# Moving the routing work, the u-row gathers and their dot products of one decoder layer to other keys

## The chip, the cores and the metric

The kernel runs on one core of a Trainium2 chip. Five engines work side by side, each with its own instruction stream: PE (TensorE, matmuls), DVE (VectorE), ACT (ScalarE), POOL (GpSimd) and SP (SyncE, which here only issues DMAs). They wait for each other and for DMAs by semaphores. The metric is the device time of one execution in microseconds (us).

## The reference, cut to what matters

The layer takes 256 tokens of width 1024 through a recurrent branch and attention, cross-attention, and then a channel mixer over 16,384 single-neuron experts. Only the mixer matters here:

```
q = (t @ w_q).reshape(T, 8, 2, 128)                 # 8 heads, two halves
s = einsum('thpd,hpnd->thpn', q, sub_keys)          # 128 sub-keys a half
s_top, i_top = top_k(s, 16)                         # then 16 of the 16 x 16 sums
best_s, pos = top_k(cand_s, 16); ids = take(cand_i, pos); gates = softmax(best_s)
act = gelu(einsum('td,ted->te', x_c, u[ids_c]), approximate=False)
y = einsum('te,ted->td', g_c * act, v[ids_c])       # 128 experts a token
```

An expert number is a pair (i, j) of sub-keys, each 0 to 127. All of it is float32.

## The kernel before, in words

**Dense stages.** Most of the mixer is computed for all experts: the u stage multiplies all u rows with the tokens, key by key (a key j is 128 experts), and the v stage multiplies all v rows with the weighted activations, again key by key. In both, SP loads a key's 512 KB (`raw`, four slots), ACT copies it to a high part (`split_high`), DVE subtracts to get the low part (`split_low`), and PE multiplies both. DVE's iteration j splits key j + 4, and a slot is free again when PE is done with its key, so ACT and DVE run at most four keys ahead. In the u stage ACT then applies GeLU (`gelu`) to what PE leaves in PSUM.

**Routing.** DVE finds the experts of each token meanwhile: four parts a head (`route_part`; two top-16 of 128, one of 256, one of index arithmetic), 8 heads, two tiles of 128 tokens, 64 parts in all. The first 14 come ahead of the u stage; part n of the others comes in DVE's iteration `part_key(n)`, 1.5 keys apart. When a batch of heads is done (`BATCHES`), ACT takes the exponentials (`gate_exp`, `batch_key` + 2, which needs another activation table than GeLU) and DVE makes the gates and addresses (`gates`, `batch_key` + 4).

**Where the gates go.** Three ways, by token. For most, POOL scatters the gates with indirect DMAs (L517, 128 elements each) into a zeroed map in HBM (`wmap`): 16 scatters for each of 8 heads of tile 0, then 4 for each head of tile 1. From the second head on, a head's first scatter of a set waits until those of the head before have landed. SP (and, for the first two blocks, POOL) reads the map back as `wblk`, and DVE weighs the activations with it (`weigh`); the first `weigh` stands in iteration 124 of the u stage. For 48 tokens, PE places the gates by one-hot matrices: 12 groups of 4 (`onehots_i` on DVE and `onehots_j` on ACT two keys ahead, `route` on PE behind key `ROUTE0` + 3g, `place` on DVE in the same key), after PE has transposed the routing rows behind key `WEAVE` (80), which waits for the last gates.

**Sparse tokens.** For 48 tokens the v side is done by gathering single v rows (48 gathers of 128 rows, `vg`, three buffers) and adding them with a weight on DVE (`sparse_fma`, from v iteration 12 on). For 16 of them the u side is done so too: 16 gathers of 128 u rows (`u_rows` on POOL, 512 KB each, buffers `ug0` and `ug1`), each followed by one dot product with the tokens (`u_dot` on DVE). `u_rows(0)` waits for the index lists, which go through HBM (SP, at raw keys 88 and 93), and for the tokens' rows times the gains (DVE at `XREP_KEY`, semaphore `s_xg`); from the third on each waits for the dot that frees its buffer. Before, they stand behind every second scatter of the last batch (heads 3 to 7 of tile 1), the last six behind all scatters, and the dots come at keys 92 to 120.

**Order.** Each engine's instructions run in the order written, so what waits holds all behind it. On POOL: scatters with the u gathers among them, the first two `wblk`, eight gathers of stored activations (`act_rows`), then v rows and more activation gathers in turn.

Of the kernel before, what the change touches and what calls it, by code (L numbers as in the profile page):

```python
# [22 lines left out]
P = 128  # L23
# [36 lines left out]
GRP = 4  # L60
# [20 lines left out]
BATCHES = ((0, 0, 1), (0, 1, 3), (0, 3, 5), (0, 5, PH), (1, 0, 3), (1, 3, PH))  # L81
EARLY = 2
PARTS0 = 14
WEAVE = 80
LATE0 = 76
RUN = 7
GAINS = 6
ROUTE0 = 84
RSTEP = 3
HALVES_TO = 80  # L90
XREP_KEY, DOT0 = 90, 92
NUG = 2


def build(nc, x, mem, par, wa, wx, w, keys_t, u_t, urow, v, g_row, wmap, adump, sgate, sidx, xres, xrows, out):
    ctx = ExitStack()
    with ctx:
# [189 lines left out]

        def part_key(n):

            return -(-3 * (n - PARTS0 + 1) // 2) - 1  # L290

        def set_ranks(ap, k):

# [36 lines left out]

        SPARSE = ((P - NS, NSA, 0, NDA), (P - NSB, NSB, NDA, NDB))

        def placed(j):

            return GRP * max(0, min(NGRP, (j - ROUTE0) // RSTEP + 1))

        def group_at(j):

            g, rest = divmod(j - ROUTE0, RSTEP)
            return g if rest == 0 and 0 <= g < NGRP else None  # L340

        def dot_key(c):

            return DOT0 + 15 * c // 8

        ug = (ug0, ug1)

# [4 lines left out]
        def _(sp):  # L352
# [42 lines left out]
            for j in range(4, KEYS):  # L395
                sp.wait_ge(s_ul, j - 3)
                sp.dma_start(raw[:, j // 2 % 2, j % 2], u_t[j // 2][:, j % 2]).then_inc(s_raw[j % 4], 16)
                if j == 88:
                    sp.wait_ge(s_stg, 1)
                    for far, near in ((sgate, stage_g), (sidx, stage_i)):  # L400
                        for t0, nt, c0, nc_ in SPARSE:
                            sp.dma_start(far[P * c0:P * (c0 + nc_), :].rearrange("(r t c) o -> t r (c o)", t=nt, c=nc_),
                                         near[t0:t0 + nt, :].rearrange("t (r c) -> t r c", c=nc_)).then_inc(s_sst, 16)
                if j == XREP_KEY:
                    sp.wait_ge(s_rt, TT * PH)
                    sp.wait_ge(s_xrd, 16)
                    for r in range(P // NSB):
                        sp.dma_start(xrep[NSB * r:NSB * r + NSB], xrows).then_inc(s_xrb, 16)
                    sp.dma_start(ug0[:], g_row.broadcast_to([P, D])).then_inc(s_xrb, 16)
                if j == 93:  # L410
                    sp.wait_ge(s_sst, 64)
                    for far, near in ((sgate, gate_s), (sidx, idx_v)):
                        for t0, nt, c0, nc_ in SPARSE:
                            sp.dma_start(near[:, c0:c0 + nc_],
                                         far[P * c0:P * (c0 + nc_), :].rearrange("(p c) o -> p (c o)", p=P)).then_inc(s_sbk, 16)
                if j % DUMP == 0 and j >= 3 * DUMP:
                    dump(j - 3 * DUMP, j - 2 * DUMP)
                if j == KEYS - 4:
                    dump(KEYS - 3 * DUMP, KEYS - 2 * DUMP)
# [37 lines left out]
        def _(pool):  # L457
# [41 lines left out]
            def u_rows(c):  # L499
                if c == 0:  # L500
                    pool.wait_ge(s_sbk, 64)
                    pool.wait_ge(s_xg, 1)
                if c >= NUG:
                    pool.wait_ge(s_dot, c - NUG + 1)
                nc.gpsimd.indirect_dma_start(out=ug[c % NUG][:], out_offset=None, in_=urow,
                                             in_offset=bass.IndirectOffsetOnAxis(ap=idx_v[:, NDA + c:NDA + c + 1], axis=0)).then_inc(s_ug[c % NUG], 16)

            pool.wait_ge(s_zero, 16 * NZERO)
            for b, (t, h0, h1) in enumerate(BATCHES):
                pool.wait_ge(s_gr, b + 1)  # L510
                for h in range(h0, h1):
                    for k in TILE_SETS[t]:
                        nr = SETS[k][3]
                        if h:
                            pool.wait_ge(s_sca[k], 16 * nr * h)
                        for r in range(nr):
                            nc.gpsimd.indirect_dma_start(  # L517
                                out=wmap, out_offset=bass.IndirectOffsetOnAxis(ap=set_ranks(widx, k)[:, h, r:r + 1], axis=0),
                                in_=set_ranks(gate, k)[:, h, r:r + 1], in_offset=None, compute_op=ALU.add).then_inc(s_sca[k], 16)
                            if b == len(BATCHES) - 1 and r % 2:  # L520
                                u_rows((nr * (h - h0) + r) // 2)

            for c in range(2 * (BATCHES[-1][2] - BATCHES[-1][1]), NDB):
                u_rows(c)
            for k, (_, _, _, nr) in enumerate(SETS):
                pool.wait_ge(s_sca[k], 16 * nr * PH)
            pool.wait_ge(s_sst, 64)
            for p in range(2):
                nc.gpsimd.dma_start(wblk[:, p], wm[:, WBK * p:WBK * p + WBK]).then_inc(s_wbp[p], 16)
            pool.wait_ge(s_ad, 16 * KEYS // DUMP)  # L530
            pool.wait_ge(s_ix, 1)

# [16 lines left out]
        def _(act):  # L549
# [304 lines left out]
            for j in range(KEYS):  # L854
                landed = 16 * ((j + 4) // 4 + 1)
                if j == XRT_KEY:
                    act.wait_ge(s_xd, 16)
                    act.wait_ge(s_xrd, 16)
                gelu(j)
                if j < KEYS - 4:  # L860
                    split_high(j % 4, landed, (s_um, j + 1), s_uh)
                elif j < KEYS - 1:
                    split_high(j % 4, landed, (s_um, j + 1), s_vh, second=True)
                if exps < len(BATCHES) and j == batch_key(exps) + 2:
                    gate_exp(exps)
                    exps += 1
                if j == WEAVE:
                    act.wait_ge(s_kt, 1)
                    nc.scalar.activation(kt3[:], acc[:, 2, 0:3 * P].rearrange("p (a t) -> p a t", a=3)[:, :, HT:HT + OT], ACT.Copy).then_inc(s_kte, 1)
                    act.wait_ge(s_kte, 1)  # L870
                if group_at(j + 2) is not None:
                    onehots_j(group_at(j + 2))
                if j == KEYS - 3:
                    act.wait_ge(s_gw, NGRP)
                    for p in range(2):
                        a_high(p)

            split_high(3, 16 * (KEYS // 4 + 1), (s_um, KEYS), s_vh, second=True)
            for p in (2, 3):
                a_high(p)  # L880
            act.wait_ge(s_dot, NDB)
            nc.scalar.activation(aw_s[:, NDA:NSD], dots[:], ACT.Gelu).then_inc(s_dg, 1)
            act.wait_ge(s_fx, KEYS - ROUTE0)
            for j in range(KEYS - 4):
                split_high(j % 4, 16 * (KEYS // 4 + (j + 4) // 4 + 1), (s_vm, j + 1), s_vh, second=True)
                if j % 2 and (j + 7) // 2 < NWB:
                    a_high((j + 7) // 2)
            warm_sqrt()
            act.wait_ge(s_Wl, NWB)
            for c in range(DC):  # L890
# [27 lines left out]
        def _(dve):  # L918
# [339 lines left out]
            def place(g):  # L1258

                dve.wait_ge(s_gm, g + 1)  # L1260
                j0, c = ROUTE0 + RSTEP * g, P + group_token(g)
                dve.wait_ge(s_ua, j0)
                w = acc[:, 2 + g % 2].rearrange("p (t j) -> p j t", t=GRP)
                aw = act_w[:, :, c:c + GRP]
                V.tensor_copy(aw[:, j0:KEYS], w[:, j0:KEYS])
                V.tensor_tensor(aw[:, 0:j0], w[:, 0:j0], aw[:, 0:j0], ALU.mult).then_inc(s_gw, 1)
# [59 lines left out]
                    V.tensor_scalar(to, vg[:, c % NVG], w, None, ALU.mult).then_inc(s_fma, 1)  # L1326

            def u_dot(c):
                dve.wait_ge(s_ug[c % NUG], 16 * (c // NUG + 1))
                row = ug[c % NUG]  # L1330
# [3 lines left out]
            parts, batches, dot = PARTS0, EARLY, 0  # L1334
            for j in range(KEYS):
                if j < HALVES_TO:
                    split_low_halves(j % 4, s_ul, (s_uh, j + 5))
# [1 line left out]
                    split_low(j % 4, s_ul, (s_uh, j + 5))  # L1339
                elif j < KEYS - 1:  # L1340
                    split_low(j % 4, s_vl, (s_vh, j + 5 - KEYS), second=True)
                if batches < len(BATCHES) and j == batch_key(batches) + 4:
                    gates(batches)
                    batches += 1
                if parts < 4 * TT * PH and j == part_key(parts):
# [11 lines left out]
                if j == DOT0 - 1:  # L1357
                    dve.wait_ge(s_sbk, 64)
                    V.tensor_scalar(idx_a[:], idx_v[:, 0:NDA], float(NSA), tcol[:, 2:3], ALU.mult, ALU.add).then_inc(s_ix, 1)
                if dot < NDB and j == dot_key(dot):  # L1360
                    u_dot(dot)
                    dot += 1
                if group_at(j + 2) is not None:
                    onehots_i(group_at(j + 2))
                if j == KEYS - 4:
# [12 lines left out]
            for j in range(KEYS - 4):  # L1378
# [6 lines left out]
                split_low(j % 4, s_vl, (s_vh, j + 5), second=True)  # L1385
                if j % 2 == 0 and 4 <= (j + 6) // 2 < NWB:
                    a_low((j + 6) // 2)
                if c < NSD and j == fma_step(c):
                    sparse_fma(c)
                    c += 1  # L1390
# [432 lines left out]
```

## Time and profile before

| | us |
|---|---|
| median of three runs | 987.94 (986.53 to 989.32) |
| the profiled execution | 987.83, its span 986.0 |
| u stage, on PE | 280.7 to 667.7 |
| v stage, on PE | 667.7 to 972.2 |
| busy: PE, DVE, ACT, POOL | 952.0, 803.7, 558.3, 421.6 |

The profile covers one execution; its times count from the first instruction. A line as L517 is a line of the kernel. A tile name left of an arrow is written, right of it is read. Durations of matmuls are modelled and overlap; the distances between their starts are sharper.

### The profile page before, as it was taken

Reading aid. Unit: us, or ns where it says so; the run is one execution under the profiler, and the core shown is the slowest. Engines: PE = TensorE matmul, PEld = TensorE weight load, DVE = VectorE, ACT = ScalarE, POOL = GpSimd, SP = SyncE. Lnnn points to the kernel's source line nnn. Section 1 sums busy time; section 2 is a strip of 40 time slices with the busy share of each in tenths; the row PEclk is TensorE's granted clock in tenths of the full one; section 3 lists DMA queues with packets and bytes.
Section 4 is the critical chain, followed back from the end, with each engine's and each line's share of the span. In section 5 each row is a group of like instructions: output and inputs, shape, how many; then the busy total and the mean of one; then the engine's idle time right before and its main releaser. Section 6 shows DMA issues by size and latency. Waiting matters only on the chain.

```text
span 986.0 us, 18901 instructions
## 1 busy us (share of the span) xinstructions
PE 952.0 (97%) x7255; PEld 927.2 (94%) x7255; DVE 803.7 (82%) x1557; ACT 558.3 (57%) x1005; POOL 421.6 (43%) x283
## 2 busy tenths in 40 slices
PE   8999999999999999999999598999999999999997
PEld 8897899999999999999999598999999999999997
DVE  5988776447999999999976377867798999989887
ACT  7675445645556555555566454755555555555455
POOL 1001001000588888888885677216365223222210
PEclk9999999999999999999999889999999999999999
DMA  9699635444557777878888588878999999999992
GB/s 318 207 334 327 235 136 204 131 129 129 175 110 192 186 195 190 197 192 202 198 223 229 126 240 228 295 233 285 307 368 347 354 342 358 336 354 358 364 314 86
DMA packets 130812, 239.90 MB, mean 243 GB/s; under 512 B 33904, under 2 KB 82800, under 8 KB 130368
## 3 DMA queue, kind: packets, MB, share of 16 engines
q1 hardware_dynamic: 96944, 204.60, 61.6%
q0 software_dynamic: 33376, 34.00, 15.6%
q8 instruction: 31, 0.51, 0.2%
q10 hardware_dynamic: 432, 0.57, 0.2%
q14 instruction: 29, 0.24, 0.1%
HBM read 223.72 MB, written 14.88 MB: 242 GB/s over the span
## 4 chain that ended last, share of the span: by engine, by line
PE 60%; POOL 26%; issue 6%; DMA 4%; DVE 3%; ACT 1%; ACTq 0%; DVEq 0%; POOLq 0%
POOL wmap L517 26%; PE acc L1720 11%; PE bank L1720 10%; PE acc L1479 10%; PE bank L1721 5%; PE acc L1721 5%; PE acc L1461 4%; DMA wmap<-gate,widx 3%; PE bank L1669 2%; PE bank L1668 2%; PE bank L1670 2%; PE acc L1462 2%; PE acc L1465 1%; DVE wsp L930 1%; PE bank L1577 1%
## 5 line engine op out<-in xcount | busy, mean ns | idle before, releaser
L517 POOL DMA_INDIRECT wmap<-gate,widx x160 | 277.3, 1733 | 95.6 <-issue 47.0
L803 ACT ACTIVATE hl<-raw 128x1024 fp32r<-128x1024 f32 x192 | 203.5, 1061 | 78.9 <-PE bank L1721 41.3
L1668 PE MATMUL bank<-xt,hl 128*128 128x240 f32 x768 | 213.9, 279 | 3.8 <-DVE hl L1187 3.5
L1670 PE MATMUL bank<-xt,hl 128*128 128x240 f32 x768 | 212.2, 276 | 0.0
L1669 PE MATMUL bank<-xt,hl 128*128 128x240 f32 x768 | 212.2, 276 | 0.0
L1180 DVE TENSOR_TENSOR hl<-raw,hl 128x1024 fp32r<-128x1024 f32 x132 | 161.7, 1225 | 56.0 <-ACT hl L803 55.5
L1668 PEld LDWEIGHTS bank<-xt,hl 128*128 128x128 f32 x768 | 146.3, 191 | 4.7 <-ACT act_s L814 4.3
L1669 PEld LDWEIGHTS bank<-xt,hl 128*128 128x128 f32 x768 | 146.2, 190 | 0.0
L1670 PEld LDWEIGHTS bank<-xt,hl 128*128 128x128 f32 x768 | 146.1, 190 | 0.0
L544 POOL DMA_INDIRECT vg<-v,idx_v x48 | 64.7, 1348 | 164.3 <-DVE acc_s L1324 143.4
L1720 PE MATMUL acc<-whl,hl 128*128 128x416 f32 x380 | 121.3, 370 | 0.0
L1720 PE MATMUL bank<-whl,hl 128*128 128x416 f32 x380 | 120.9, 368 | 0.0
L809 ACT ACTIVATE act_w<-bank 128x208 f32<-128x208 f32 (+12 forms) x128 | 42.8, 334 | 128.9 <-PE bank L1670 128.7
L554 ACT ACTIVATE wsp<-wraw 128x2048 fp32r<-128x2048 f32 x35 | 66.9, 1913 | 57.0 <-PE acc L1462 26.5
L930 DVE TENSOR_TENSOR wsp<-wraw,wsp 128x2048 fp32r<-128x2048 f32 x34 | 77.9, 2290 | 25.9 <-ACT wsp L554 25.6
L1721 PE MATMUL bank<-whl,hl 128*128 128x208 f32 x380 | 98.1, 258 | 0.0
L1721 PE MATMUL acc<-whl,hl 128*128 128x208 f32 x380 | 97.9, 258 | 0.0
L1479 PE MATMUL acc<-xt,wsp 128*128 128x256 f32 x672 | 83.9, 285 | 0.1
L1479 PEld LDWEIGHTS acc<-xt,wsp 128*128 128x128 f32 x672 | 81.6, 191 | 0.7 <-issue 0.4
L1187 DVE TENSOR_TENSOR hl<-raw,hl 128x512 fp32r<-128x512 f32 x120 | 76.6, 687 | 1.9 <-ACT hl L803 0.8
L1668 PE MATMUL bank<-xt,hl3u 128*128 128x240 f32 x256 | 70.8, 277 | 1.7 <-DVE hl3u L1187 1.7
L1721 PEld LDWEIGHTS acc<-whl,hl 128*128 128x128 f32 x380 | 72.5, 191 | 0.0
(299 smaller groups left out, 2169.8 us busy)
## 6 DMA issues: line engine op xcount, KB each, us to landing
raw<-u_t SPq DMA_DIRECT2D x128, 512.0 KB, 4.6
raw<-v SPq DMA_DIRECT2D x128, 512.0 KB, 5.9
wmap<-zeros SPq DMA_DIRECT2D x5, 2048.0 KB, 11.2
wblk<-wmap SPq DMA_DIRECT2D x62, 160.0 KB, 5.9
wraw<-w_in SPq DMA_DIRECT2D x9, 1024.0 KB, 9.4
wraw<-w_pq SPq DMA_DIRECT2D x8, 1024.0 KB, 5.3
wraw<-w_ck SPq DMA_DIRECT2D x4, 1024.0 KB, 8.9
wraw<-w_cv SPq DMA_DIRECT2D x4, 1024.0 KB, 6.2
```

The source lines that it names most:

```text
L517: nc.gpsimd.indirect_dma_start(out=wmap, out_offset=bass.IndirectOffsetOnAxis(ap=set_ranks(widx, k)[:, h, r:r + 1], axis=0), in_=set_ranks ...
L554: nc.scalar.activation(wsp[:, u % 2, 0], wraw[:, u % WRAW], ACT.Copy).then_inc(s_wh, 1)
L803: nc.scalar.activation(eslot(k, 0, second), raw[:, k // 2, k % 2], ACT.Copy).then_inc(ready, 1)
L930: V.tensor_tensor(wsp[:, u % 2, 1], wraw[:, u % WRAW], wsp[:, u % 2, 0].bitcast(F32), ALU.subtract).then_inc(s_wl, 1)
L1180: V.tensor_tensor(eslot(k, 1, second), raw[:, k // 2, k % 2], eslot(k, 0, second).bitcast(F32), ALU.subtract).then_inc(ready, 1)
L1187: last = V.tensor_tensor(eslot(k, 1, False)[:, q], raw[:, k // 2, k % 2, q], eslot(k, 0, False)[:, q].bitcast(F32), ALU.subtract)
L1479: last = pe.matmul(dst, a, b, start=(c == c0 and n == 0), stop=(c == c1 - 1 and n == 2))
L1668: pe.matmul(dst, uh[:, c], xt[:, c, 0, 0:UT], start=(c == 0), stop=False)
L1669: pe.matmul(dst, uh[:, c], xt[:, c, 1, 0:UT], start=False, stop=False)
L1670: last = pe.matmul(dst, ul[:, c], xt[:, c, 0, 0:UT], start=False, stop=(c == DC - 1))
L1720: pe.matmul(both, vh[:, q], whole, start=first, stop=False, skip_group_check=True)
L1721: last = pe.matmul(both[:, 0], vl[:, q], whole[:, 0], start=False, stop=False, skip_group_check=True)
```

## The change

Parts come every 1.6 keys in place of 1.5. The exponentials of a batch come one key behind its last part (two before), the gates three (four before). The transposes move from key 80 to 83, the groups to 87 + 2.75g (84 + 3g before). SP stores and reloads the lists at raw keys 92 and 97 (88 and 93), the product with the gains moves from key 90 to 91. Twelve u gathers stand behind the scatters 2, 5, 8, ... of tile 1 (counted from 0), their dots at keys 97 to 122; the other four stand behind the first two `wblk`, use one buffer, and have their dots in the v stage at iterations 1, 4, 7 and 10. ACT's GeLU of the dots moves to v iteration 20.

```diff
-WEAVE = 80
+WEAVE = 83
-ROUTE0 = 84
-RSTEP = 3
+ROUTE0 = 87
-XREP_KEY, DOT0 = 90, 92
+XREP_KEY = 91
+DOT_KEYS = (97, 100, 103, 106, 108, 110, 112, 114, 116, 118, 120, 122)
+LATE_DOTS = (1, 4, 7, 10)
+U_AFTER = (2, 5, 8, 11, 13, 15, 17, 20, 22, 25, 28, 31)
...
         def part_key(n):
-            return -(-3 * (n - PARTS0 + 1) // 2) - 1
+            return -(-8 * (n - PARTS0 + 1) // 5) - 1
...
+        def group_key(g):
+            return ROUTE0 + 11 * g // 4
...
+        def uslot(c):
+            return c % NUG if c < len(DOT_KEYS) else 0
...
-                if j == 88:
+                if j == 92:
                     sp.wait_ge(s_stg, 1)
...
-                if j == 93:
+                if j == 97:
                     sp.wait_ge(s_sst, 64)
...
-                if c >= NUG:
+                if c >= len(DOT_KEYS):
+                    pool.wait_ge(s_dot, c)
+                elif c >= NUG:
                     pool.wait_ge(s_dot, c - NUG + 1)
...
-                            if b == len(BATCHES) - 1 and r % 2:
-                                u_rows((nr * (h - h0) + r) // 2)
-
-            for c in range(2 * (BATCHES[-1][2] - BATCHES[-1][1]), NDB):
-                u_rows(c)
+                            if t and nr * h + r in U_AFTER:
+                                u_rows(U_AFTER.index(nr * h + r))
...
                 nc.gpsimd.dma_start(wblk[:, p], wm[:, WBK * p:WBK * p + WBK]).then_inc(s_wbp[p], 16)
+            for c in range(len(DOT_KEYS), NDB):
+                u_rows(c)
...
-                if exps < len(BATCHES) and j == batch_key(exps) + 2:
+                if exps < len(BATCHES) and j == batch_key(exps) + 1:
                     gate_exp(exps)
...
+                    act.wait_ge(s_dot, len(DOT_KEYS))
                     for p in range(2):
                         a_high(p)
...
-                if batches < len(BATCHES) and j == batch_key(batches) + 4:
+                if batches < len(BATCHES) and j == batch_key(batches) + 3:
                     gates(batches)
...
-                if dot < NDB and j == dot_key(dot):
-                    u_dot(dot)
-                    dot += 1
+                if j in DOT_KEYS:
+                    u_dot(DOT_KEYS.index(j))
...
+                if j in LATE_DOTS:
+                    u_dot(len(DOT_KEYS) + LATE_DOTS.index(j))
```

## Rows read from the trace of the kernel before

**Rows 1.** Page, parts 1 and 5: busy; count, total us, mean ns, idle before.

```profile
PE 952.0 (97%) x7255; PEld 927.2 (94%) x7255; DVE 803.7 (82%) x1557; ACT 558.3 (57%) x1005; POOL 421.6 (43%) x283
...
L517 POOL DMA_INDIRECT wmap<-gate,widx x160 | 277.3, 1733 | 95.6 <-issue 47.0
```

**Rows 2.** Waits of the u stage: waiter, releaser; us in total, times, longest.

```profile
DVE ug L1331 <- DMA ug<-u,idx_v: 19.5, 5, 12.7
...
ACT krow L795 <- DVE krow L1219: 1.9, 3, 1.2
```

**Rows 3.** Timeline of PE: start, duration, line, operation; in brackets idle before.

```profile
508.67 0.55 PE L1703 MATMUL acc<-ident,krow 128*128 128x128 f32 x3 [1.57 <-DVE widx L1245]
...
569.32 2.08 PE L1693 MATMUL acc<-oh_j,oh_i 128*128 128x128 f32 x8 [13.50 <-DVE oh_i L1254]
...
578.41 0.27 PE L1668 MATMUL bank<-xt,hl3u 128*128 128x240 f32 x1
...
581.10 1.05 PE L1693 MATMUL acc<-oh_j,oh_i 128*128 128x128 f32 x8
581.91 0.36 PE L1668 MATMUL bank<-xt,hl 128*128 128x240 f32 x1
...
602.18 1.93 PE L1693 MATMUL acc<-oh_j,oh_i 128*128 128x128 f32 x8 [3.00 <-DVE oh_i L1254]
...
607.49 0.27 PE L1668 MATMUL bank<-xt,hl3u 128*128 128x240 f32 x1
...
667.70 0.35 PE L1720 MATMUL acc<-whl,hl 128*128 128x416 f32 x1
...
708.54 0.36 PE L1720 MATMUL acc<-whl,hl 128*128 128x416 f32 x1
```

**Rows 4.** Windows: stretch, busy PE, PEld, DVE, ACT, POOL, then clock, DMA, GB/s.

```profile
280.00:504.00 224.00, 218.53 (x1934) 217.12 (x1933) 214.37 (x616) 128.81 (x257) 190.46 (x111) 1.00 0.78 192
...
602.00:604.00 2.00, 1.82 (x9) 1.82 (x10) 2.00 (x4) 0.00 (x0) 1.73 (x1) 0.59 0.61 145
```

**Rows 5.** Timeline of POOL: scatters of tile 1, then the start of the v stage.

```profile
522.72 1.55 POOL L517 DMA_INDIRECT wmap<-gate,widx  x1 [0.30 <-issue]
529.63 1.55 POOL L517 DMA_INDIRECT wmap<-gate,widx  x1 [5.36 <-DMA wmap<-gate,widx]
...
540.21 1.85 POOL L517 DMA_INDIRECT wmap<-gate,widx  x1 [3.41 <-DMA wmap<-gate,widx]
...
552.11 1.55 POOL L517 DMA_INDIRECT wmap<-gate,widx  x1 [4.34 <-DMA wmap<-gate,widx]
...
670.85 1.03 POOL L535 DMA_INDIRECT aw_s<-adump,idx_a  x1 [25.75 <-DMA adump<-act_s]
...
683.90 0.98 POOL L544 DMA_INDIRECT vg<-v,idx_v  x1 [0.30 <-issue]
```

**Rows 6.** Tiles: u gathers' ns; landings of late u, first v, first weight blocks.

```profile
L505 POOL DMA_INDIRECT ug<-u,idx_v x16: 939/1416/1820, 555.8 to 642.2; - x16
...
DMA to landing us min/median/max: 4.8/6.5/7.5
...
DMA to landing us min/median/max: 7.6/8.1/9.6
...
DMA to landing us min/median/max: 6.0/6.1/6.2
```

**Rows 7.** Timeline of DVE: a head's parts, the product, the first sparse sum.

```profile
481.28 0.17 DVE L1211 TENSOR_SCALAR posu<-topi 128x16 uint32<-128x16 uint32 x1
...
497.39 0.17 DVE L1211 TENSOR_SCALAR posu<-topi 128x16 uint32<-128x16 uint32 x1
...
541.42 1.22 DVE L1356 TENSOR_TENSOR xrep<-xrep,ug 128x1024 f32<-128x1024 f32 x1
...
702.94 0.76 DVE L1326 TENSOR_SCALAR acc_s<-vg,w_s 128x1024 f32<-128x1024 f32 x1
...
704.01 1.22 DVE L1180 TENSOR_TENSOR hl<-raw,hl 128x1024 fp32r<-128x1024 f32 x1
```

More of the change, by code:

```diff
@@ L331, in build, with uslot_use @@
         SPARSE = ((P - NS, NSA, 0, NDA), (P - NSB, NSB, NDA, NDB))
+        def group_key(g):
+            return ROUTE0 + 11 * g // 4
         def placed(j):
-            return GRP * max(0, min(NGRP, (j - ROUTE0) // RSTEP + 1))
+            return GRP * sum(1 for g in range(NGRP) if group_key(g) <= j)
         def group_at(j):
[L339 to L344, printed above, removed]
+            return next((g for g in range(NGRP) if group_key(g) == j), None)
+        def uslot(c):
+            return c % NUG if c < len(DOT_KEYS) else 0
+        def uslot_use(c):
+            return sum(1 for k in range(c + 1) if uslot(k) == uslot(c))
         ug = (ug0, ug1)
@@ L502, in u_rows @@
                     pool.wait_ge(s_xg, 1)
-                if c >= NUG:
+                if c >= len(DOT_KEYS):
+                    pool.wait_ge(s_dot, c)
+                elif c >= NUG:
                     pool.wait_ge(s_dot, c - NUG + 1)
-                nc.gpsimd.indirect_dma_start(out=ug[c % NUG][:], out_offset=None, in_=urow,
-                                             in_offset=bass.IndirectOffsetOnAxis(ap=idx_v[:, NDA + c:NDA + c + 1], axis=0)).then_inc(s_ug[c % NUG], 16)
+                nc.gpsimd.indirect_dma_start(out=ug[uslot(c)][:], out_offset=None, in_=urow,
+                                             in_offset=bass.IndirectOffsetOnAxis(ap=idx_v[:, NDA + c:NDA + c + 1], axis=0)).then_inc(s_ug[uslot(c)], 16)
             pool.wait_ge(s_zero, 16 * NZERO)
@@ L880, in _ @@
                 a_high(p)
-            act.wait_ge(s_dot, NDB)
-            nc.scalar.activation(aw_s[:, NDA:NSD], dots[:], ACT.Gelu).then_inc(s_dg, 1)
             act.wait_ge(s_fx, KEYS - ROUTE0)
@@ L887, in _ @@
                     a_high((j + 7) // 2)
+                if j == 20:
+                    act.wait_ge(s_dot, NDB)
+                    nc.scalar.activation(aw_s[:, NDA:NSD], dots[:], ACT.Gelu).then_inc(s_dg, 1)
             warm_sqrt()
@@ L1260, in place @@
                 dve.wait_ge(s_gm, g + 1)
-                j0, c = ROUTE0 + RSTEP * g, P + group_token(g)
+                j0, c = group_key(g), P + group_token(g)
                 dve.wait_ge(s_ua, j0)
@@ L1328, in u_dot @@
             def u_dot(c):
-                dve.wait_ge(s_ug[c % NUG], 16 * (c // NUG + 1))
-                row = ug[c % NUG]
+                dve.wait_ge(s_ug[uslot(c)], 16 * uslot_use(c))
+                row = ug[uslot(c)]
                 V.scalar_tensor_tensor(row[:], row[:], 1.0, xrep[:], ALU.mult, ALU.mult,
                                        accum_out=dots[:, c:c + 1]).then_inc(s_dot, 1)
-            parts, batches, dot = PARTS0, EARLY, 0
+            parts, batches = PARTS0, EARLY
             for j in range(KEYS):
@@ L1356, in _ @@
                     V.tensor_tensor(xrep[:], xrep[:], ug0[:], ALU.mult).then_inc(s_xg, 1)
-                if j == DOT0 - 1:
+                if j == XREP_KEY + 1:
                     dve.wait_ge(s_sbk, 64)
                     V.tensor_scalar(idx_a[:], idx_v[:, 0:NDA], float(NSA), tcol[:, 2:3], ALU.mult, ALU.add).then_inc(s_ix, 1)
-                if dot < NDB and j == dot_key(dot):
-                    u_dot(dot)
-                    dot += 1
+                if j in DOT_KEYS:
+                    u_dot(DOT_KEYS.index(j))
                 if group_at(j + 2) is not None:
```

## The prediction, made before the changed kernel ran

> **What bounds the kernel now.** I read the page first: TensorE is busy for 952.0 of 986.0 us [rows 1], so only its gaps can be won, and then whatever makes them. The waits of the u stage come next: DVE waited 19.5 us in five waits for u rows that POOL gathers, 12.7 us in one of them [rows 2]. TensorE's timeline says what these waits cost [rows 3]. A key of the u stage takes 2.69 us there (578.41 to 581.10) and a routing group behind it 0.81 us (581.10 to 581.91). The group behind key 96 waited 13.50 us for its one-hots, the one behind key 105 waited 3.00 us, and the transposes of the routing rows behind key 80 waited 1.57 us for the last gates. Up to key 80 the gaps are small: 224 less 218.53, 5.5 us, in one stretch of 224 us [rows 4]; DVE and TensorE have almost the same pace there, since four routing parts and six splits took 16.11 us on DVE (481.28 to 497.39) [rows 7] against six keys of 2.69 us, 16.1 us. The v stage begins at 667.70 and its key 17 at 708.54, 2.40 us a key, with no gap [rows 3]. So about 27 us of gaps lie ahead of the v stage, and the v stage itself has none to give.
>
> All times below are on the clock of the profiled execution, which took 987.8 us with a span of 986.0; the median of the runs is 987.9, the same within their scatter. About 0.3%, 3.0 us, is what a measurement can tell from no change.
>
> **Parts every 1.6 keys.** No work is removed; six keys become 6.4 for a head. DVE's 16.11 us grow by 0.4 split of some 1.2 us to 16.6 us, against 17.2 us of TensorE: 0.6 us of lead for each head, 1.8 us between two sets of gates that stand three heads apart. That is about what one set costs now (5.5 us in three sets, some 1.8 us each). Against it, the exponentials of a batch now run on ACT one key behind the batch's last part and no longer two, and ACT already waited 1.9 us in three waits for that part [rows 2]; while ACT stands, the next splits stand too. I count nothing. The ends are a gain of all 5.5 us and a loss of twice the present 1.9 us, 3.8.
>
> **Gates and transposes.** The last part moves from key 74 to 79, the last gates from 78 to 82, the transposes only from 80 to 83. TensorE waited 1.57 us with two keys between the two; with one key it is 2.69 more, and DVE has two keys without parts ahead of the gates in place of three, so it comes with about 1 us less lead: 5.2 us, 3.6 more than now. After the 3.00 us wait behind key 105 the granted clock stood at 0.59 (near the 1.2 GHz level) in the next 2 us [rows 4], and group and key took 5.31 us (602.18 to 607.49) in place of 3.50: 1.8 us. After the wait of 1.57 us it stayed full. A wait of 5.2 us brings this 1.8 us too: 5.4 us together. The ends are nothing, if DVE has caught up, and 8.
>
> **The first u gather.** It stands behind the third scatter of tile 1 and needs the index lists and the product of the gains, which DVE forms at key 91. Scatters of tile 1 start no later than now, and the third is out by 522.7, where the fourth starts now [rows 5]. The product started at 541.42 in key 90 [rows 7]. In the new order it comes 2.69 later (one key), 5.4 later (above), and 1.6 earlier (one group less has run, 0.81, and no group is placed in this key, some 0.8): 547.9, and it takes 1.22, so 549.1. POOL stands for 26 us with 29 scatters and the gathers queued behind it. Before, it scattered in this time.
>
> From there POOL is the chain. 29 scatters take 2.0 us each (1.73 mean and 0.30 of issue [rows 1]), 58.0; 12 gathers 1.72 (1.42 and 0.30 [rows 6]), 20.6. At each of seven changes of head POOL waits until the head before has landed; where no gather lies between, it now waits 5.36, 3.41 and 4.34 us [rows 5], 4.1 more than the issue, and five changes are of that kind: 20.4. The other two have a gather between; I give them 1 us each. That is 101.0 us, to 650.1 for the twelfth gather; the last scatter starts 3.7 earlier, 646.4, lands some 5.6 later (2.0 and a wait of 3.6 to 4.3), 652.0. Only then can the first blocks of weights be fetched, 6.1 us [rows 6], 658.1; weighing and splitting them takes about 2.5 us, and the v stage starts at 660.6. TensorE alone would be done sooner: from the product's key it has 37 keys of 2.69 and ten groups, some 108 us after 543, 651. The twelve dots cost nothing of their own up to key 116; the last three wait for their gathers inside this difference of 9 us. So the removed 13.5 and 3.0 us and their slow clock come back partly as a wait at the end: 660.6 against 667.70, **7.1 us won**. The ends: 19 us won, if the product is early and the landings short, and 1 lost.
>
> **Four dots in the v stage.** They use one buffer, so each gather waits for the dot before it, and now the gathers for the sparse v rows queue behind all four. Relative to the start of the v stage, DVE's split of key 17 starts at 36.3 (704.01 [rows 7]); twelve iterations earlier, at 2.40 a key, iteration 1 splits at 7.5. The dot behind it ends at 10.0. The gather of the next lands 6.5 later [rows 6], 16.5, about when iteration 4 comes to it; dot done 17.8. Landing 24.3, while iteration 7 was ready at some 23.7; dot done 25.5. With the fourth gather issued POOL is free at 27.2. Now the eight gathers of stored activations and the first of v: 13.05 us between 670.85 and 683.90 [rows 5], to 40.3, and 8.1 to land [rows 6], 48.4. In the profile of before this whole chain began at 3.15. The first sparse sum is due at 35.2 (702.94). Sum and weighing take 1.07 and the split of key 17 1.2: ready at 50.7, while TensorE wants key 17 at 40.8 (708.54): 9.9 us of wait, in which nothing else is queued for TensorE. Then again 1.8 us of slow clock: **11.7 us lost**. The v stage runs at TensorE's pace to its end, so nothing gives it back. The ends are 2 us and 15 us.
>
> A rule of the Trainium skill speaks against this term. Rows of before: the last u gathers landed in 4.8, 6.5, 7.5 us (least, median, most), the first v gathers in 7.6, 8.1, 9.6 [rows 6]. The page "DMA: Bandwidth & Descriptors", section "Anatomy of one DMA", puts a transfer from this queue at 2.0 us and its bytes over 436 GB/s, which is 3.2 us for 512 KB, an estimate by that page. By that the gathers would wait for no dot, and the v rows be there early enough that a small wait of about 2 us remained, as in the third rival. The rows don't bear it out; the sum goes by them.
>
> **Dot and one-hot keys, groups from 87 every 2.75 keys.** Twelve groups as before, 0.81 us each on TensorE, and the same instructions of DVE and ACT at other keys; the dots that now come late were the ones between which DVE waited. Nothing, with half a microsecond to either side.
>
> **Sum.** 987.8 − 7.1 + 11.7 = 992.4; I say 992.3.
>
> **Rivals.**
> *DVE arrives with lead.* If the slower pace hides the gates' 5.5 us and the transposes wait no longer than now, the product comes 10.9 us earlier and the whole POOL chain with it: 992.3 − 10.9 = 981.4, faster. For it: 0.6 us a head. Against: the exponentials moved towards their part, and one key between gates and transposes. It decides at key 83: a wait under 2 us there.
> *Shorter landings.* With 4.8 us for the late u gathers (the shortest shown), v rows at 7.6, and 3.4 us at the changes of head, the v stage starts 3.5 us earlier and its wait is 2.2 us shorter: 986.6, no change. For it: the three waits at heads lie 2 us apart, and the shortest is 3.41 [rows 5]. Against: v gathers took longer than u gathers [rows 6].
> *Fast gathers.* At 3.2 us for all gathers the v chain ends with a wait of some 2 us at full clock: 992.3 − 9.7 = 982.6. This is the time that the cited rule gives. Against: the shortest of the late u gathers took 4.8 [rows 6].
> *The gathers don't go among the scatters.* If DVE were still waiting at key 97 for its first row, 13 us would stay: the forecast plus some 7, 999. The gather lands some 7 us after the product, the dot is due six keys, 16 us, after it; I hold this for unlikely.
>
> **How the numbers follow.** Forecast 0.50 (its own range 989 to 997), lead 0.13, fast gathers 0.07, shorter landings 0.27, no weave 0.03. Faster is the second and third, 0.20; same 0.27 (the landings); slower 0.53. The range 982 to 999 leaves out the far side of the early product, and double losses.
>
> **What would show it.** Transposes behind key 83 waiting 4 to 6 us; POOL idle from 522 to about 549 ahead of its first gather; no TensorE gap between keys 87 and 117; the last scatter at about 646; v stage from 658 to 663; then one gap of TensorE of some 10 us ahead of key 16 to 18 of the v stage, released by DVE waiting at its first sparse sum for a v row. If TensorE runs through the v stage without that gap, the forecast is wrong by its largest term; if the v stage starts before 653, by its second.

## The result, and the profile after

The changed kernel takes 992.99 us (median of five runs, 989.31 to 993.41) against 987.94 us (five runs, 985.87 to 989.32): a ratio of 1.0046, with an interval of 1.0024 to 1.0069. It is slower by half a percent, near the 992.3 us forecast. The profiled execution took 993.41 us with a span of 991.6 us, 5.6 us longer than before.

| start of | before | after | difference |
|---|---|---|---|
| u stage | 280.74 | 281.23 | +0.5 |
| key 80 of tile 1 | 504.25 | 505.15 | +0.9 |
| v stage | 667.70 | 664.29 | −3.4 |
| last matmuls of the v stage | 972.19 | 978.06 | +5.9 |

So the u stage won 3.4 us and the v stage lost 9.3 (313.77 us long in place of 304.49). First the page of the changed kernel, parts 1 and 5, in the columns of [rows 1]:

```profile
PE 959.0 (97%) x7255; PEld 933.0 (94%) x7255; DVE 802.3 (81%) x1554; ACT 556.8 (56%) x1002; POOL 428.0 (43%) x283
...
L528 POOL DMA_INDIRECT wmap<-gate,widx x160 | 273.2, 1708 | 99.0 <-issue 47.8
```

The count of TensorE's instructions is the same, and its busy time grew by 7 us: the same matmuls, some of them at the lower clock. The waits of the changed kernel from 280 to 720 us (waiter, releaser; us in total, times, longest) show where it stood:

```profile
POOL ug L516 <- DVE ug L1344: 38.4, 7, 15.8
POOL ug L516 <- DVE xrep L1369: 31.2, 1, 31.2
DVE ug L1344 <- DMA ug<-u,idx_v: 20.7, 4, 8.2
...
ACT krow L806 <- DVE krow L1232: 10.2, 4, 3.6
...
PE acc L1734 <- DVE hl L1193: 6.1, 1, 6.1
...
PE acc L1717 <- DVE widx L1258: 5.2, 1, 5.2
```

DVE waits for u rows as long as before (20.7 against 19.5 us in [rows 2]), only later. ACT's wait for routing parts has grown from 1.9 to 10.2 us. New is the 31.2 us that POOL stands for the product. TensorE's timeline of the changed kernel has one line for each loss:

```profile
521.22 0.90 PE L1717 MATMUL acc<-ident,krow 128*128 128x128 f32 x3 [5.15 <-DVE widx L1258]
...
642.40 0.57 PE L1682 MATMUL bank<-xt,hl3u 128*128 128x240 f32 x1 [2.69 <-DVE hl3u L1193]
...
653.27 0.57 PE L1682 MATMUL bank<-xt,hl 128*128 128x240 f32 x1 [3.70 <-DVE hl L1193]
...
664.29 0.35 PE L1734 MATMUL acc<-whl,hl 128*128 128x416 f32 x1
...
711.75 0.72 PE L1734 MATMUL acc<-whl,hl 128*128 128x416 f32 x1 [6.15 <-DVE hl L1193]
```

The 13.50 and 3.00 us ahead of the one-hot groups in [rows 3] are gone: no group waits any more. In their place stand 5.15 us at the transposes, 2.69 and 3.70 us in the last keys of the u stage, and 6.15 us in the v stage. Each of the four is followed by slow matmuls: the transposes took 0.90 us where they took 0.55. Windows of the changed kernel (columns of [rows 4]; the clock stands behind POOL's share) around the transposes show the same:

```profile
280.00:504.00 224.00, 218.41 (x1930) 216.76 (x1929) 209.87 (x601) 125.20 (x254) 188.66 (x113) 1.00 0.77 194
...
516.00:518.00 2.00, 0.07 (x1) 0.00 (x0) 1.96 (x2) 2.00 (x5) 1.70 (x2) 1.00 0.88 197
...
522.00:524.00 2.00, 2.00 (x11) 2.00 (x11) 0.42 (x1) 0.29 (x1) 0.00 (x0) 0.50 0.47 78
524.00:526.00 2.00, 2.00 (x12) 2.00 (x11) 0.00 (x0) 0.00 (x0) 0.00 (x0) 0.50 0.96 311
526.00:528.00 2.00, 2.00 (x19) 2.00 (x19) 0.00 (x0) 1.11 (x3) 0.00 (x0) 0.96 0.92 207
```

TensorE stood from 516 to 521; after that it is busy without a break, but until 526 with 11 or 12 matmuls in 2 us in place of 19, at a granted clock of 0.50 (1.2 GHz). The first line says that the small gaps up to key 80 are what they were: 224 less 218.41, 5.6 us, against 5.5 in [rows 4].

DVE's timeline of the changed kernel shows what the two waits in the last keys of the u stage come from, the tenth and the eleventh dot (keys 118 and 120):

```profile
639.98 1.23 DVE L1344 SCALAR_TENSOR_TENSOR ug<-ug,xrep 128x1024 f32<-128x1024 f32 x1 [8.16 <-DMA ug<-u,idx_v]
...
650.85 1.23 DVE L1344 SCALAR_TENSOR_TENSOR ug<-ug,xrep 128x1024 f32<-128x1024 f32 x1 [7.12 <-DMA ug<-u,idx_v]
```

POOL's timeline of the changed kernel, from the third scatter of tile 1 to the first sparse v row:

```profile
519.97 1.55 POOL L528 DMA_INDIRECT wmap<-gate,widx  x1 [0.31 <-issue]
552.75 1.13 POOL L516 DMA_INDIRECT ug<-u,idx_v  x1 [31.23 <-DVE xrep L1369]
...
559.93 1.54 POOL L528 DMA_INDIRECT wmap<-gate,widx  x1 [4.16 <-DMA wmap<-gate,widx]
...
648.52 1.55 POOL L528 DMA_INDIRECT wmap<-gate,widx  x1 [0.30 <-issue]
...
652.22 1.17 POOL L538 DMA_DIRECT2D wblk<-wmap  x2 [0.85 <-DMA wmap<-gate,widx]
...
673.78 1.75 POOL L516 DMA_INDIRECT ug<-u,idx_v  x1 [15.85 <-DVE ug L1344]
683.38 0.95 POOL L516 DMA_INDIRECT ug<-u,idx_v  x1 [7.85 <-DVE ug L1344]
689.77 1.68 POOL L516 DMA_INDIRECT ug<-u,idx_v  x1 [5.44 <-DVE ug L1344]
691.75 1.74 POOL L546 DMA_INDIRECT aw_s<-adump,idx_a  x1 [0.30 <-issue]
...
704.52 0.95 POOL L555 DMA_INDIRECT vg<-v,idx_v  x1 [0.30 <-issue]
```

In [rows 5] the stored activations were fetched from 670.85 and the v rows from 683.90, 3.15 and 16.20 us into the v stage. Now three late gathers, each behind the dot before it, stand ahead of them, and they come at 27.5 and 40.2 us. The chain of waits of the changed kernel (start, us, what) walks the same road back:

```profile
642.93 7.89 DMA ug<-u,idx_v
...
673.78 8.07 DMA ug<-u,idx_v
...
704.52 4.79 DMA vg<-v,idx_v
709.40 0.75 DVE acc_s L1339
```

All three are landings of gathers: that of the eleventh dot's rows, near the end of the u stage, that of a late dot's, and that of the first v row. The tiles of the changed kernel: landings of the u gathers after 650 us, of the first v rows, and the first weighing.

```profile
DMA to landing us min/median/max: 4.2/7.4/8.1
...
DMA to landing us min/median/max: 4.8/5.1/5.9
...
L1322 DVE TENSOR_TENSOR act_w<-act_w,wblk x2: 483/484/485, 658.3 to 658.7; 128x320 f32<-128x320 f32 x2
```

### The profile page after: what moved, and what is told of

Read it like the earlier page. It is cut to its first block, busy times and chain, and to the rows that moved or that the text cites. A ratio compares the mean times of both kernels' runs of the same rounds, so it can differ in the third digit from the quotient of the medians.

```text
span 991.6 us, 18892 instructions
## 1 busy us (share of the span) xinstructions
PE 959.0 (97%) x7255; PEld 933.0 (94%) x7255; DVE 802.3 (81%) x1554; ACT 556.8 (56%) x1002; POOL 428.0 (43%) x283
## 4 chain that ended last, share of the span: by engine, by line
PE 70%; DVE 16%; DMA 4%; ACT 3%; POOL 3%; issue 3%; ACTq 0%; DVEq 0%; POOLq 0%
PE acc L1493 14%; PE acc L1734 9%; PE bank L1734 9%; PE bank L1682 5%; PE bank L1683 5%; PE bank L1684 5%; DVE hl L1200 5%; PE bank L1735 4%; PE acc L1735 4%; PE acc L1475 4%; PE acc L1476 2%; DMA wmap<-gate,widx 2%; DVE hl3u L1200 2%; DMA ug<-u,idx_v 2%; POOL wmap L528 1%
## 5 line engine op out<-in xcount | busy, mean ns | idle before, releaser
L528 POOL DMA_INDIRECT wmap<-gate,widx x160 | 273.2, 1708 | 99.0 <-issue 47.8
L555 POOL DMA_INDIRECT vg<-v,idx_v x48 | 74.2, 1545 | 137.6 <-DVE acc_s L1337 129.8
L820 ACT ACTIVATE act_w<-bank 128x208 f32<-128x208 f32 (+11 forms) x128 | 43.0, 336 | 125.4 <-PE bank L1684 125.2
L862 ACT ACTIVATE whl<-act_w 128x416 fp32r<-128x416 f32 x64 | 35.1, 551 | 76.3 <-DVE act_w L1322 76.1
```

The costliest lines, as they stand in the source:

```text
L528: nc.gpsimd.indirect_dma_start(out=wmap, out_offset=bass.IndirectOffsetOnAxis(ap=set_ranks(widx, k)[:, h, r:r + 1], axis=0), in_=set_ranks ...
L555: nc.gpsimd.indirect_dma_start(out=vg[:, c % NVG], out_offset=None, in_=v, in_offset=bass.IndirectOffsetOnAxis(ap=idx_v[:, c:c + 1], axis= ...
```

## The experiments

Each alters the changed kernel in one or two places, except where it says otherwise; the kernel before, run beside them, took 988.2 and 988.0 us. The changed kernel was not run beside them, so a difference from its 992.99 us is one between sittings. A time is a median, a trace one execution, which can lie some us off the median; where that matters, the text says so.

**Groups from key 85.** Two more keys between the last gates and the transposes.

```diff
-WEAVE = 83
+WEAVE = 85
```

> The changed kernel with the transposes behind key 85 in place of 83, nothing else. Theory (the transposes stand one key too close to the gates; their wait of 5.15 us and the slow clock of key 84 push the product of key 91 and with it the whole POOL chain): two keys, 5.4 us, cover the wait; TensorE's gap behind the transposes under 0.5 us, no slow key, the first u gather near 545.5 in place of 552.8, v stage from 657, same gap in the v stage; 986 us. Rival (the v stage's start is set by the scatters' own landings and not by the product): the gap goes, the v stage still starts at 664, 993 us.

It took 985.08 us, 0.9973 [0.9953, 0.9994] of the time before, in ten runs from 982.01 to 991.25. In the profiled one (988.88 us, 3.8 above the median) the transposes started at 521.07 without a wait, and the first gather at 544.91 in place of 552.75; POOL now waited for the index lists, which landed about 0.2 us behind the product. Of these 7.8 us only 4.9 reached the v stage, which started at 659.43, later than expected: four of the last dots waited for their gathers, and behind the first of them (6.17 us) one group stood, as this line of TensorE's timeline in that run shows.

```profile
621.88 2.08 PE L1707 MATMUL acc<-oh_j,oh_i 128*128 128x128 f32 x8 [4.24 <-DVE oh_i L1267]
```

So the wait at key 83 delays POOL's chain by its length and the slow matmuls behind it. In this execution the next wait on the chain hides part of what its removal wins; by the medians the kernel gained 7.9 us, all of it, so the hidden part is shown for this execution only.

**u gathers later among the scatters.**

```diff
-U_AFTER = (2, 5, 8, 11, 13, 15, 17, 20, 22, 25, 28, 31)
+U_AFTER = (11, 13, 15, 17, 19, 21, 23, 25, 27, 29, 30, 31)
```

> The changed kernel with the twelve u gathers behind scatters 11, 13, 15, ... 29, 30, 31 of tile 1 in place of 2, 5, 8, ... Theory (the first gather held POOL for 31 us with 29 scatters behind it): POOL scatters through from 520, waits for the product only some 5 us, the last scatter starts near 630 in place of 648.5, the v stage starts at 653 to 655 set by TensorE's own keys, the gap in the v stage stays near 6 us; 982 to 984 us. Rival (the late dots wait for landings and for each other, whatever the order on POOL): v stage from 662 to 665, 991 to 994 us.

982.62 us, 0.9941 [0.9919, 0.9962]. POOL scatters while it waited before, and stands 3.77 us for the product, not 31.23. TensorE's timeline of that run:

```profile
520.91 0.90 PE L1717 MATMUL acc<-ident,krow 128*128 128x128 f32 x3 [5.16 <-DVE widx L1258]
...
652.66 0.35 PE L1734 MATMUL acc<-whl,hl 128*128 128x416 f32 x1
...
700.22 0.71 PE L1734 MATMUL acc<-whl,hl 128*128 128x416 f32 x1 [6.49 <-DVE hl L1193]
```

The transposes wait as before it, the two waits of 2.69 and 3.70 us are gone, and the v stage starts 11.6 us earlier. The gap of the v stage is untouched. The place of the gathers among the scatters, not their number, cost these 11.6 us.

**Stored activations ahead of the late gathers.**

```diff
-            for c in range(len(DOT_KEYS), NDB):
-                u_rows(c)
+            u_rows(len(DOT_KEYS))
...
-            act_rows(0, ACTB)
+            act_rows(0, 4)
+            u_rows(len(DOT_KEYS) + 1)
+            act_rows(4, ACTB)
+            u_rows(len(DOT_KEYS) + 2)
...
+                if c == NVG - 1:
+                    u_rows(len(DOT_KEYS) + 3)
```

> The changed kernel with POOL's order at the start of the v stage altered: four gathers of stored activations behind the first late u gather, four behind the second, the first three v gathers ahead of the fourth; the same transfers in all. Theory (the v gathers are late because they queue behind four u gathers that each wait for a dot): the first v row lands by 30 us after the start of the v stage, before it is due at 35; no gap near key 17; 984 us. Rival (the late rows share the DMA engines with the loads of the v stage, so the rows come late in any order): a gap of 4 us or more stays, 989 us or more.

987.1 us, 0.9991 [0.9968, 1.0014]: no difference from the kernel before, and between the two theories. The first v row was fetched 21.9 us into the v stage (683.40, from a start at 661.53) in place of 40.2, and no sparse sum waited for it. But the dots, which come every third iteration, now wait for their own gathers; DVE's timeline of that run:

```profile
680.64 1.23 DVE L1348 SCALAR_TENSOR_TENSOR ug<-ug,xrep 128x1024 f32<-128x1024 f32 x1 [4.03 <-DMA ug<-u,idx_v]
...
697.92 1.23 DVE L1348 SCALAR_TENSOR_TENSOR ug<-ug,xrep 128x1024 f32<-128x1024 f32 x1 [3.01 <-DMA ug<-u,idx_v]
```

TensorE stood 2.61 us behind the second, again with slow matmuls after it. With this order too somebody waits; whether another order of four dots within ten iterations on one buffer would do without was not tried.

**The late dots spread over the v stage.**

```diff
-LATE_DOTS = (1, 4, 7, 10)
+LATE_DOTS = (1, 20, 40, 60)
...
-            for c in range(len(DOT_KEYS), NDB):
-                u_rows(c)
+            u_rows(len(DOT_KEYS))
...
+                if c in (4, 12, 20):
+                    u_rows(len(DOT_KEYS) + 1 + (4, 12, 20).index(c))
...
-                if j == 20:
+                if j == 70:
```

> The changed kernel with its four dots of the v stage at iterations 1, 20, 40 and 60 in place of 1, 4, 7 and 10, the u gathers of the last three behind the v gathers 4, 12 and 20 on POOL, and ACT's gelu of these dots at key 70. Theory (the gap ahead of v key 17 comes from POOL, which stands for the dots before it may fetch stored activations and sparse v rows): the gap of 6.15 us and the slow clock behind it vanish, the v stage is as long as in the kernel before (304.5 us in place of 313.8), and the kernel takes about 984 us. Rival (the u gathers cost the v stage in whatever place, because their 512 KB hold up the v rows and blocks of weights): the waits move to sparse sums behind these gathers, with gaps of 2 us and more, 988 us or more.

981.79 us, 0.9934 [0.9911, 0.9956]. One window of that run over the v stage, in the columns of [rows 4]:

```profile
661.00:971.00 310.00, 310.00 (x2083) 308.28 (x2082) 276.44 (x336) 170.46 (x211) 120.60 (x83) 1.00 0.93 335
```

TensorE is busy for all 310 us at full clock. The same dots and gathers cost the v stage nothing in these places; what cost was where they stood in POOL's queue and in DVE's order, which this edit moves together. The rival falls.

**The kernel before, with its dots alone moved.** No other part of the change.

```diff
-            return DOT0 + 15 * c // 8
+            return 98 + 3 * c // 2
```

> The kernel before with one line altered: its sixteen dots at keys 98 to 120, 1.5 keys apart, in place of 92 to 120. Theory (the gap of 13.5 us came only from the first dot standing ahead of its gather, which POOL reaches at 555.8): the gap behind key 96 and its slow clock go, 16 us; later dots wait for gathers for some 5 us in all, the v stage starts at 652 to 656; 973 to 976 us. Rival (the gathers among the scatters set the pace, and what the first dot does not wait the later ones do): v stage from 663, 983 us or more.

982.62 us, 0.9941 [0.9917, 0.9966]: the rival was right, within half a us. The 13.50 us went, and came back in pieces. TensorE's timeline of the profiled execution, which took 986.70 us, the longest of six, with the v stage from 666.60:

```profile
586.23 1.64 PE L1693 MATMUL acc<-oh_j,oh_i 128*128 128x128 f32 x8 [3.11 <-DVE oh_i L1254]
...
600.04 1.77 PE L1693 MATMUL acc<-oh_j,oh_i 128*128 128x128 f32 x8 [2.96 <-DVE oh_i L1254]
...
614.94 2.08 PE L1693 MATMUL acc<-oh_j,oh_i 128*128 128x128 f32 x8 [4.05 <-DVE oh_i L1254]
...
629.51 1.16 PE L1693 MATMUL acc<-oh_j,oh_i 128*128 128x128 f32 x8 [2.53 <-DVE oh_i L1254]
```

Together 12.65 us there, and some 4 us less by the median: the gathers on POOL come as late as before (the first at 556.1), so DVE waits a little for several of them. Moving the one constant still beat the whole change.

**Groups from key 85 and later gathers together.**

```diff
-WEAVE = 83
+WEAVE = 85
...
-U_AFTER = (2, 5, 8, 11, 13, 15, 17, 20, 22, 25, 28, 31)
+U_AFTER = (11, 13, 15, 17, 19, 21, 23, 25, 27, 29, 30, 31)
```

> The changed kernel with two single edits together: routing groups from key 85 (as the run with that edit alone, 985.1 us) and the u gathers from the eleventh scatter on (alone 982.6 us). Theory (POOL's chain from the product to the last scatter is what both shorten, so they add): the product is done about 5 us earlier, POOL no longer stands for it, the v stage starts at 645 to 647 (652.7 less 6 to 7), the gap of some 6 us ahead of v key 17 is untouched, and the kernel takes about 976 us. Rival (the last dots then wait for their gathers in the u stage, as they did with the groups from key 85 alone, where one waited 6.2 us): v stage from 651 or later, 981 us or more.

973.96 us, 0.9856 [0.9823, 0.9889], 2 us better than the theory. The v stage starts at 644.98, no transpose and no dot of the u stage waits; the gap in the v stage is 5.19 us. The rival falls: the two edits add (7.9 and 10.4 us alone, 19.0 together), since each takes other waits from TensorE, the one at the transposes and the two at the last dots, with the slow matmuls behind them.

**Exponentials two keys behind their part.** With the groups from key 85, to be set beside the first experiment.

```diff
-                if exps < len(BATCHES) and j == batch_key(exps) + 1:
+                if exps < len(BATCHES) and j == batch_key(exps) + 2:
...
-                if batches < len(BATCHES) and j == batch_key(batches) + 3:
+                if batches < len(BATCHES) and j == batch_key(batches) + 4:
```

> The changed kernel with the groups from key 85, and with the exponentials of a batch two keys behind its last routing part in place of one, and the gates four keys behind in place of three; to be set beside the run with the groups from key 85 alone (985.1 us). Theory (ACT stands for DVE's last part, and DVE's next splits stand for ACT): ACT's waits for routing parts fall from 10 us to about 2, TensorE's small gaps at keys 16 to 57 of tile 1 from 5.3 us to 2 or 3, and the kernel takes about 982 us. Rival (these gaps are DVE's own pace at the gates, whoever waits): the gaps stay at 5 us and the time at 985; with the last gates a key later the transposes may even wait again, up to 2.7 us, 988.

980.83 us, 0.9926 [0.9899, 0.9953]. The window of that run over tile 1's first keys:

```profile
280.00:504.00 224.00, 222.54 (x1980) 221.89 (x1980) 215.15 (x614) 128.09 (x260) 188.53 (x111) 1.00 0.79 198
```

The gaps are 1.5 us in place of 5.6, key 80 starts at 499.15, and ACT's wait for parts is gone from the waits. The theory held, and the gain at key 80 was twice what it asked. The edit moves the gates on DVE with the exponentials; the two were not parted.

**The routing parts' pace undone.** All else as changed, the groups from key 83 too.

```diff
-            return -(-8 * (n - PARTS0 + 1) // 5) - 1
+            return -(-3 * (n - PARTS0 + 1) // 2) - 1
...
-                if exps < len(BATCHES) and j == batch_key(exps) + 1:
+                if exps < len(BATCHES) and j == batch_key(exps) + 2:
...
-                if batches < len(BATCHES) and j == batch_key(batches) + 3:
+                if batches < len(BATCHES) and j == batch_key(batches) + 4:
```

> The changed kernel (993.0 us) with the pace of the routing parts undone: every 1.5 keys, the exponentials two keys and the gates four keys behind a batch's last part, all else as changed. The prediction gave this pace nothing for the small gaps and a loss of 5.4 us for the transposes behind key 83. Theory: the gaps up to key 80 stay at some 5.5 us in place of 5.3, the transposes wait no longer than 1 us since the last gates then stand at key 78, the product is done some 5 us earlier, the v stage starts near 659 to 660 as with the groups from key 85, and the kernel takes about 985 us. Rival (the slower pace did save time even with the exponentials a key nearer): the gaps grow by 2 us or more, 988 us or more.

980.81 us, 0.9922 [0.9899, 0.9945], 4 us better than the theory. The window of that run up to key 80:

```profile
280.00:504.00 224.00, 218.81 (x1937) 217.40 (x1936) 214.33 (x616) 128.06 (x257) 190.15 (x112) 1.00 0.79 192
```

The gaps stay (5.2 us), the transposes stand at 515.18 without a wait, and the product starts at 542.25 in place of 550.66. The v stage starts at 653.95, 10.3 us earlier: 8.4 from the product, the rest from behind it. Without this one part, the pace with the two offsets that go with it, the change would have been 0.8% faster than the kernel before.

**All edits.** First three: these lines, and the other lines of the spread dots as above.

```diff
-WEAVE = 83
+WEAVE = 85
...
-LATE_DOTS = (1, 4, 7, 10)
-U_AFTER = (2, 5, 8, 11, 13, 15, 17, 20, 22, 25, 28, 31)
+LATE_DOTS = (1, 20, 40, 60)
+U_AFTER = (11, 13, 15, 17, 19, 21, 23, 25, 27, 29, 30, 31)
```

> The changed kernel with all three edits: groups from key 85, u gathers from the eleventh scatter on, and the dots of the v stage spread over iterations 1, 20, 40 and 60. Theory (three separate costs that add): v stage from 645 to 647, then 318.3 us from there to the end of the span as in the kernel before, and 1.8 us around the span: 965 to 968 us. Rival (one of the removed waits comes back in another place, at the dots of the u stage or behind the late gathers): 975 us or more.

965.76 us, 0.9768 [0.974, 0.9795], as the theory said; v stage from 645.05. Against that kernel, the next has the exponentials moved as well, and the first gathers two places earlier:

```diff
-U_AFTER = (11, 13, 15, 17, 19, 21, 23, 25, 27, 29, 30, 31)
+U_AFTER = (9, 12, 15, 17, 19, 21, 23, 25, 27, 29, 30, 31)
...
-                if exps < len(BATCHES) and j == batch_key(exps) + 1:
+                if exps < len(BATCHES) and j == batch_key(exps) + 2:
...
-                if batches < len(BATCHES) and j == batch_key(batches) + 3:
+                if batches < len(BATCHES) and j == batch_key(batches) + 4:
```

> The run with all three edits (965.8 us), with the exponentials two keys and the gates four keys behind a batch's last part as well, and the first gathers among the scatters two places earlier (behind the tenth scatter), since the product of the gains comes earlier. Theory (the small gaps at keys 16 to 56 of tile 1 go as they did with that edit alone, where key 80 started 5.7 us earlier, and POOL has slack enough): v stage from 639 to 641 in place of 645.1, no gap in it, 959 to 962 us. Rival (POOL's chain of scatters to the first blocks of weights now ends last): the last scatter at 620 or later, the v stage no earlier than 643, 964 us or more.

962.14 us, 0.9735 [0.9707, 0.9763]: the best version, faster than both kernels. The v stage starts at 639.65, as expected. Its page, part 1:

```profile
PE 949.1 (99%) x7255; PEld 923.2 (96%) x7255; DVE 800.7 (83%) x1554; ACT 556.1 (58%) x1002; POOL 443.2 (46%) x283
```

TensorE is busy for 949.1 of 961.0 us. It ended 0.1 us above what was expected: from the start of the v stage to the end of the span it takes 321.4 us, 3 more than the 318.3 of before. A window over most of that stage (640 to 952 us) has TensorE idle for 1.3 us in all; where the rest goes was not tried.

## Why the prediction was right, step by step

*The span.* The two large terms were 7.1 won and 11.7 lost, a loss of 4.6; they measured 3.4 and 9.3, a loss of 5.9. Both were too large, by 3.7 and 2.4 us, and the errors nearly cancel; that the time came within 1 us is luck; its parts did not.

*Parts every 1.6 keys: nothing.* Confirmed, 5.6 us of gaps against 5.5. But the zero is two effects: the slower pace gives 4 us of lead, and the exponentials and gates one key nearer to their part take it back. ACT's waits (10.2 us against 1.9) fit that ACT stands for DVE and DVE's next splits for ACT; the runs moved exponentials and gates together, so which of the two costs is argued. With both moved back the gaps fell to 1.5 us; with the old pace too they were 5.2. Both ends that the prediction gave (5.5 won, 3.8 lost) were needed to see it.

*Transposes: a wait of 5.2 us and slow clock.* Measured 5.15. The slow clock cost some 2.5 us rather than 1.8: the transposes 0.35 more, and key 84 took 4.86 us in place of 2.69. The product stood at 550.7 to 551.9, where 549.1 was said, 2.8 us late. Some 1.6 of it are this and key 80 itself, 0.9 us later; for most of the rest, the 0.8 us that a key without a group to place should save did not come, since DVE stood 0.91 us for ACT's split there. Two runs without this wait, the groups from key 85 and the pace undone, were 7.9 and 12.2 us faster than the changed kernel by their medians; in the second TensorE still waits 1.44 and 5.24 us at the last dots, the first of them without slow matmuls behind it.

*POOL's chain: 101 us, last scatter at 646.4.* It started at 648.52, 95.8 us after the first gather (97.3 in the working), and the first weights were fetched at 652.22, where 652.0 stands in the sum. The waits at a change of head that the working had at 3.4 to 5.4 us measured 4.16, 3.24, 1.42, 2.94, 4.28 and 4.22. That the sum fits is luck in part: POOL also waited 6.4 us for three dots that had to free a buffer (0.88, 4.23 and 1.30), which the working left out, while the changes of head, the gathers (1.20 us in the mean, 1.42 said) and the scatters (1.66, 1.73 said) were shorter. Weighing at 658.3 fits a v stage from 660.6.

*The last three dots cost nothing: this step failed.* By the prediction they wait inside the 9 us that TensorE has to spare against POOL. Two of them did wait (8.16 and 7.12 us on DVE), and TensorE's waits behind them, 2.69 and 3.70, fit into that. What was left out is the slow clock behind each: keys 122 to 126 took 24.75 us, where five keys take 13.45, so 6.39 of waits brought 4.9 more, nearly all of it slow matmuls. Without these 11.3 us TensorE would have reached the v stage at 653.0, 7.6 us ahead of POOL's 660.6; with them it came at 664.29, 3.7 us behind, and that is what is missing in the gain. It is also outside the 658 to 663 that were named as a sign. The run with later gathers bears this out: it has no such waits and starts its v stage at 652.66.

*Four dots in the v stage: 11.7 us.* The mechanism and its place were right: POOL is free for the stored activations at 27.5 (27.2 said), the first v row is fetched at 40.2 (40.3 said), and one gap stands in the v stage, released by DVE behind its first sparse sum. The term that was mis-sized is the landing of that row: 8.1 us, from the first v rows of before, where it landed in 4.8 to 5.9. So the split was ready at 47.5, not 50.7, and the wait 6.15, not 9.9. The slow clock behind it cost 2.7 us (keys 17 and 18 took 4.61 and 2.85 us, key 16 8.72 with the wait) and not 1.8. The four late u gathers landed in 7.4, 8.1, 4.2 and 7.9 us, where the working had 6.5 for each. The rival of shorter landings was right about the v rows, but not about the late u gathers nor the tenth and eleventh of the u stage (8.9 and 7.9 us), and the time stayed with the forecast. The spread dots show that the term is this chain: without it TensorE is busy for 310 of 310 us.

The rival of fast gathers put 3.2 us on every landing, an estimate by the Trainium skill, page "DMA: Bandwidth & Descriptors", section "Anatomy of one DMA". The trace differs, with 4.2 us for the shortest late u gather and 4.8 for the shortest of the first v rows. The price of this rival was also off: with 3.2 us in the prediction's own chain the dots are done at 24.3, POOL is free at 26.0, the v row lands at 42.3 and the split is ready at 44.6, a wait of 3.8 us and not some 2.

## What to carry to other kernels

A wait that is taken from TensorE by asking for a transfer earlier or later comes back where the queue that issues the transfer stands for something else: follow the queue in order, its place decides more than the number of transfers. Price a short wait of TensorE with the slow matmuls behind it, here 1.6 to 3 us behind each of four waits of 2.7 us and more, before calling it hidden in a slack of that size. And where an edit moves two steps against each other, a zero may be a gain and a loss that can be parted.

## What the runs showed of the hardware beyond what was expected

The clock does not fall with every wait. After TensorE's wait of 1.57 us in the kernel before the matmuls kept their speed; after the waits of 2.69, 3.70, 5.15 and 6.15 us in the changed kernel they did not. After that of 5.15 us there were 11 or 12 matmuls in 2 us in place of 19, at 0.50 until 526 us, with the next two microseconds at 0.96. The length of the wait alone does not decide: the run of the kernel before with its dots moved kept the full clock behind its wait of 2.53 us (first line), the one with the exponentials two keys behind their part lost it behind one of 1.94 us, which ended at 628.38 (second line; columns of [rows 4]).

```profile
629.00:631.00 2.00, 1.49 (x13) 1.49 (x14) 2.00 (x5) 0.71 (x1) 0.14 (x1) 1.00 0.74 147
...
629.00:631.00 2.00, 2.00 (x13) 2.00 (x13) 0.70 (x2) 2.00 (x5) 1.70 (x2) 0.57 0.95 172
```

Landings of the same 512 KB gather differ, and in three stretches they were shorter where the DMA engines were less busy. In the kernel before the first v rows took 7.6 to 9.6 us in a stretch (683 to 693 us) with the engines 0.94 busy at 331 GB/s; in the changed kernel they took 4.8 to 5.9 us in a stretch (704 to 714 us) that TensorE's wait fell into, 0.74 busy at 245 GB/s; with the dots spread and no wait, 5.9 to 8.7 (679 to 689 us, 0.88 at 312 GB/s). That the queue empties because TensorE stands, and the tile loads with it, fits these three; it was not tried by itself. The first two stretches, in the columns of [rows 4]:

```profile
683.00:693.00 10.00, 10.00 (x69) 9.94 (x68) 6.78 (x8) 5.63 (x7) 5.98 (x6) 1.00 0.94 331
...
704.00:714.00 10.00, 3.85 (x20) 3.54 (x19) 4.34 (x7) 2.44 (x3) 7.87 (x8) 0.82 0.74 245
```
